# A two-block float32 transformer on one core: rounded products of four stages walk their 272 columns in pieces instead of in order

## The chip, the cores and the metric

The kernel runs on one core of a Trainium2 chip. The metric is the time of one execution on the device in microseconds (us). Before the change the median of two runs is 1358.34 us (1358.07 to 1358.61).

## The reference, cut to what matters

Two transformer blocks of two layers each run over the same 272 tokens (16 meta tokens and 256 of the input), with 1024 features. All operands are float32.

```python
h = concatenate([meta, x])                       # 272 x 1024
for i in range(2):                               # first block
    h = h + (gla_mixer, dsa_mixer)[i](rmsnorm(h, norm_mix[i]), ...)
    h = h + swiglu(rmsnorm(h, norm_ffn[i]), ffn_w_in[i], ffn_w_out[i])
x = rmsnorm(h, norm_final)[:, 16:]
h = concatenate([meta_2, x])                     # second block, again 272 tokens
h = h + retention_mixer(rmsnorm_2(h, g), ret_w_in, ...)
h = h + swiglu_2(rmsnorm_2(h, g), w1, w3, w2)
h = h + mla_mixer(rmsnorm_2(h, g), ..., k_shared, v_shared)
h = h + swiglu_2(rmsnorm_2(h, g), w1, w3, w2)
out = rmsnorm_2(h, final_g)[:, 16:]
```

Nearly all the arithmetic is in projections `hn @ w`, where `hn` is a normed 272 x 1024 matrix, and in the products of the feed-forward layers (hidden size 2816).

## The kernel before

**Layout.** Activations are kept with features on the 128 partitions and tokens along the columns: `xx` holds a normed input as eight tiles (`k` = 0 to 7) of 128 features by 272 tokens, and `aa` holds second operands (the input of an output projection, the hidden state of a feed-forward layer) in the same way. A tile's row is 320 elements long, of which 272 are used.

**Split products.** Every float32 factor `v` is split into a rounded part `hi` (type fp32r) and a rest `lo = v - hi`, also rounded. `Split` names the two halves of such a pair. A product is then three matmuls for each `k` that add into the same PSUM bank: `hi` weights by `hi` columns (line 589), `hi` weights by `lo` columns (line 590), `lo` weights by `hi` columns (line 591). In each the 128x128 weights are the stationary operand (tiles `uh` and `ul`) and the 272 tokens are the moving one. This is `product`. A *unit* is eight such weight tiles, 128 output features in all; one call of `product` takes one unit, so it issues 24 matmuls of 272 columns. A product with only `hi` weights (unit 0, lines 568 and 570) is a special case. In two feed-forward layers (`PAIRED`, f = 1 and 3) lines 584 and 586 take `hi` and `lo` columns in one matmul of 512: line 586 reads two runs of 256 columns that lie far apart, line 584 reads 512 columns that lie next to each other.

**Stages.** `norm_x(i)` is the `Split` of the i-th normed input. In order of time:

- i = 0: the projections of gated linear attention (GLA), `chunk` over gate, keys, queries, values and r;
- i = 1: `ffn(0, ...)`, 22 columns of units for the gate and 22 for the up projection;
- i = 2 and 3: sparse attention (DSA) and its feed-forward layer, with 256 columns in most products;
- i = 4: the projections of retention: 16 for queries and keys, 16 for values, 16 for the gate;
- i = 5: `ffn(2, ...)`, 44 units;
- i = 6 and 7: latent attention (MLA) and the last feed-forward layer, with 256 columns.

Of these, i = 0, 1, 4 and 5 take all 272 columns. The second product of each feed-forward layer reads `aa` through `ffn_y(f)`.

**Order and queues.** Each engine's program is written out by hand, in one block per engine. Weights come from HBM on SyncE's queue into three `raw` buffers; ScalarE rounds them into `uh` (line 1188), VectorE subtracts into `ul` (line 1785). Four PSUM banks (`lin`) take the products in turn, four more (`aux`) the small ones. VectorE or ScalarE empties a bank (line 1797, for instance) once the last matmul of its product has raised the semaphore `s_mm`, and `take` makes TensorE wait for that before the bank is used again. No semaphore is raised within a product, so nothing reads a bank between its 24 matmuls.

**What the change touches.** The class `Split`, the function `norm_x`, and in `product` the three matmuls of lines 589 to 591:

```python
e.matmul(ps[:, 0:n1 - n0], hi[:, k, :], x.hi[:, k0 + j, n0:n1], start=first and j == 0, stop=False)
e.matmul(ps[:, 0:n1 - n0], hi[:, k, :], x.lo[:, k0 + j, n0:n1], start=False, stop=False)
i = e.matmul(ps[:, 0:n1 - n0], lo[:, k, :], jh[k0 + j] if x.joined else x.hi[:, k0 + j, n0:n1], ...)
```

Small products that the rows below speak of: line 917 is the attention output of one head (plain float32; three products, the last of which writes two runs of 64 PSUM columns that lie 128 apart), line 992 is a score product of retention (plain float32).

Of the kernel before, what the change touches and what calls it, by code (L numbers as in the profile page):

```python
# [56 lines left out]
class Seen:  # L57


    def __init__(self, e):  # L60
        self.e, self.top = e, {}
# [46 lines left out]
class Split:  # L108


    def __init__(self, pair, s_hi, s_lo, base=0, joined=False):
        self.joined = joined
        self.pair, self.hi, self.lo = pair, pair[:, 0], pair[:, 1]
        self.s_hi, self.s_lo, self.base = s_hi, s_lo, base


def build(nc, A, out):
    ctx = ExitStack()
    with ctx:
# [3 lines left out]
        def sem(name):  # L123
            return ctx.enter_context(nc.semaphore(name))
# [10 lines left out]
        _, xx, xx_flat = parts_of("xx", KC)  # L135
# [4 lines left out]
        joined = [xx_flat[:, 2 * ROW * k + GAP_X:2 * ROW * k + GAP_X + 2 * TQ] for k in range(KC)]  # L140
        jh, jl = [j[:, 0:TQ] for j in joined], [j[:, TQ:2 * TQ] for j in joined]
# [29 lines left out]
        class Arena:  # L171
            def __init__(self):
                self.at = 0
# [319 lines left out]
        s_hi, s_lo, s_pad = sem("s_hi"), sem("s_lo"), sem("s_pad")  # L493
# [8 lines left out]
        s_xh, s_xl, s_sq, s_ssq = ([sem(f"{n}{i}") for i in range(8)] for n in ("s_xh", "s_xl", "s_sq", "s_ssq"))  # L502
# [28 lines left out]
                             "s_res1", "s_out", "s_qs"))  # L531

        def norm_x(i):
            return Split(xx, s_xh[i], s_xl[i], 0, i == 7)

        def ffn_y(i):
            return Split(aa, s_fh, s_fl, FC * i)
# [14 lines left out]
        def _(e):  # L552
            w = Seen(e)
            n_mm = n_ax = 0

            def product(ps, x, n0, n1, k0=0, first=True, last=True, part=None, pair=False, ahead=0):

                nonlocal n_mm  # L560
                u = len(unit_end) + ahead
                hi, lo = unit_hi(u), unit_lo(u)
                ks = range(unit_n(u)) if part is None else part
                if u in PACKED:
                    w.wait_ge(s_lo, u + 1)
                    for k in ks:
                        w.wait_ge(x.s_hi, x.base + k + 1)
                        e.matmul(ps[:, 0:n1 - n0], hi[:, k, :], x.hi[:, k, n0:n1], start=k == 0, stop=False)
                        w.wait_ge(x.s_lo, x.base + k + 1)
                        i = e.matmul(ps[:, 0:n1 - n0], hi[:, k, :], x.lo[:, k, n0:n1], start=False, stop=k == KC - 1)  # L570
                    i.then_inc(s_mm, 1)
                    n_mm += 1
                    unit_end.append(n_mm)
                    return
                if u != HALVED:
                    w.wait_ge(s_hi, u + 1)
                    w.wait_ge(s_lo, u + 1)
                for j, k in enumerate(ks):
                    if u == HALVED:
                        w.wait_ge(*((s_lo, u + 1) if k >= 4 else (s_lo_half, 1)))  # L580
                    w.wait_ge(x.s_hi, x.base + k0 + j + 1)
                    w.wait_ge(x.s_lo, x.base + k0 + j + 1)
                    if pair and x.joined:
                        e.matmul(ps[:, :], hi[:, k, :], joined[k0 + j], start=first and j == 0, stop=False)  # L584
                    elif pair:
                        e.matmul(ps.rearrange("p (a n) -> p a n", a=2), hi[:, k, :], x.pair[:, :, k0 + j, n0:n1],  # L586
                                 start=first and j == 0, stop=False)
                    else:
                        e.matmul(ps[:, 0:n1 - n0], hi[:, k, :], x.hi[:, k0 + j, n0:n1], start=first and j == 0, stop=False)  # L589
                        e.matmul(ps[:, 0:n1 - n0], hi[:, k, :], x.lo[:, k0 + j, n0:n1], start=False, stop=False)  # L590
                    i = e.matmul(ps[:, 0:n1 - n0], lo[:, k, :], jh[k0 + j] if x.joined else x.hi[:, k0 + j, n0:n1],  # L591
                                 start=False, stop=last and j == len(ks) - 1)
                i.then_inc(s_mm, 1)
                n_mm += 1
                if part is None or ks[-1] == unit_n(u) - 1:
                    unit_end.append(n_mm)
# [62 lines left out]
            def small(key, by, steps=1):  # L659
                return aux.take(w, key, by, steps)  # L660
# [60 lines left out]
            ps = small("gain0", "D")  # L721
# [13 lines left out]
            for k in range(KC):  # L735
# [3 lines left out]
                ps = (lin if k < 4 else aux).bank(key)  # L739
                w.wait_ge(s_x[k // 4], 32)  # L740
                for n in (1, 2):
                    i = turned(ps, k, n)
# [8 lines left out]
            x = norm_x(0)  # L751
# [48 lines left out]
            ps = small(("n", 0), "D")  # L800
# [4 lines left out]
            ps = small("gain1", "D")  # L805
# [11 lines left out]
            for s in range(16):  # L817
                if s == 10:

                    ps = lin.take(w, ("gr", 2), "D")  # L820
# [31 lines left out]
            x = norm_x(2)  # L852
# [70 lines left out]
            for c in range(4):  # L923
                chunk(("di", c), "D", x, NM, T)
                if c == 0:
                    ps = small("dw8", "D")
                    w.wait_ge(s_dki, 1)
                    for b in range(2):
                        i = e.transpose(ps[:, b * P:(b + 1) * P], d_wT[:, b * P:(b + 1) * P], ident)
# [41 lines left out]
            x = norm_x(4)  # L971
# [93 lines left out]
            x = norm_x(6)  # L1065
# [55 lines left out]
            x = norm_x(7)  # L1121
            together([(3, "g", 0), (3, "g", 1)], x, NM, T, None, True)
            total(("n", 7), "A", s_ssq[7], KC - 1, ssq[0], TQ)
            ps = small("tokens", "A")
            for b in range(2):
                i = e.matmul(ps[:, b:b + 1], ssq[0][:, b * P:(b + 1) * P], ones[:, 0:1], start=True, stop=True)
# [1760 lines left out]
```

## Time and profile before

| | |
|---|---|
| median of two runs | 1358.34 us (1358.07 to 1358.61) |
| span of the profiled execution, first to last instruction | 1356.6 us |
| TensorE matmul busy | 1350.0 us, 100% |
| TensorE weight load busy | 1289.1 us, 95% |
| VectorE, ScalarE, GpSimd busy | 1010.7, 709.1, 295.4 us |
| granted TensorE clock, mean | 0.999 of full speed |
| read from HBM | 226.80 MB, 168 GB/s over the span |

The profiled execution has its span and no separate time; the runs lie 1.5 to 2.0 us above that span, and their median 1.74 us.

The profile's rows name the engine (PE is a TensorE matmul, PEld its weight load, DVE is VectorE, ACT ScalarE, POOL GpSimd), the line of the kernel, the operation, output and input tiles, shapes, and count. Busy time counts each instruction from start to end. Matmuls overlap in the pipeline, so that a row's duration (0.29 us) is much longer than the time from one start to the next (0.12 us); it is the starts that tell the rate.

### The profile page before, as it was taken

What the parts mean: (1) busy time and instruction counts of PE and PEld (TensorE: products, weight loads), DVE (VectorE), ACT (ScalarE), POOL (GpSimd) and SP (SyncE); (2) the same over time, 40 slices, a digit from 0 to 9 for tenths busy, and PEclk for the clock granted to TensorE, in tenths of its full rate; (3) what the DMA queues carried; (4) which work ended last, traced back from release to release, by engine and by line L of the source; (5) the groups of instructions that cost most, each with busy time, mean ns of one, the idle gap of its engine ahead of it and who ended that gap; (6) DMA issues with size and microseconds to landing.
All of it is one profiled execution on the core that took longest, in us unless ns stands there. A gap on an engine that the chain in (4) does not pass through costs nothing.

```text
span 1356.6 us, 24729 instructions
## 1 busy us (share of the span) xinstructions
PE 1350.0 (100%) x9873; PEld 1289.1 (95%) x9873; DVE 1010.7 (75%) x1613; ACT 709.1 (52%) x1167; POOL 295.4 (22%) x313
## 2 busy tenths in 40 slices
PE   9999999999999999999999999999999999999998
PEld 9999999999999888899999999999999999988886
DVE  6788766656987988778877876766557885898843
ACT  7565544434756555544444664544435565655543
POOL 1136000023152000132355744000023533120000
PEclk9999999999999999999999999999999999999999
DMA  8334665665443655565543455555554553566552
GB/s 279 125 125 158 191 192 185 190 186 162 136 157 126 214 190 194 170 197 181 163 134 125 155 186 158 185 174 171 170 172 150 183 161 121 172 199 189 189 184 77
DMA packets 220457, 229.72 MB, mean 169 GB/s; under 512 B 13664, under 2 KB 207704, under 8 KB 220344
## 3 DMA queue, kind: packets, MB, share of 16 engines
q1 hardware_dynamic: 219232, 226.24, 52.1%
q10 hardware_dynamic: 1112, 1.90, 0.6%
q8 instruction: 80, 1.31, 0.4%
q14 instruction: 33, 0.27, 0.1%
HBM read 226.80 MB, written 1.33 MB: 168 GB/s over the span
## 4 chain that ended last, share of the span: by engine, by line
PE 99%; DMA 0%; issue 0%; DVE 0%; ACT 0%; ACTq 0%; DVEq 0%
PE ps L591 28%; PE ps L589 21%; PE ps L590 20%; PE ps L586 8%; PE ps L584 6%; PE ps L1148 2%; PE ps L1147 2%; PE ps L1146 1%; PE ps L650 1%; PE ps L649 1%; PE ps L651 1%; PE ps L917 1%; PE ps L787 1%; PE ps L992 1%; PE ps L775 0%; PE ps L1080 0%
## 5 line engine op out<-in xcount | busy, mean ns | idle before, releaser
L1188 ACT ACTIVATE uh<-raw 128x1024 fp32r<-128x1024 f32 (+4 forms) x452 | 446.8, 999 | 441.4 <-PE ps L591 380.5
L1785 DVE TENSOR_TENSOR ul<-raw,uh 128x1024 fp32r<-128x1024 f32 (+3 forms) x448 | 529.8, 1190 | 132.7 <-PE ps L591 84.6
L591 PE MATMUL ps<-xx,ul 128*128 128x272 f32 (+1 forms) x2136 | 609.3, 285 | 0.0
L589 PE MATMUL ps<-xx,uh 128*128 128x272 f32 (+1 forms) x1448 | 422.8, 292 | 0.0
L590 PE MATMUL ps<-xx,uh 128*128 128x272 f32 (+1 forms) x1448 | 413.8, 286 | 0.0
L591 PEld LDWEIGHTS ps<-xx,ul 128*128 128x128 f32 x2136 | 401.3, 188 | 0.0
L589 PEld LDWEIGHTS ps<-xx,uh 128*128 128x128 f32 x1448 | 272.3, 188 | 3.0 <-issue 1.7
L590 PEld LDWEIGHTS ps<-xx,uh 128*128 128x128 f32 x1448 | 272.6, 188 | 0.8
L591 PE MATMUL ps<-aa,ul 128*128 128x272 f32 (+1 forms) x920 | 260.6, 283 | 0.0
L589 PE MATMUL ps<-aa,uh 128*128 128x272 f32 (+1 forms) x788 | 228.6, 290 | 0.0
L590 PE MATMUL ps<-aa,uh 128*128 128x272 f32 (+1 forms) x788 | 226.7, 288 | 0.0
L591 PEld LDWEIGHTS ps<-aa,ul 128*128 128x128 f32 x920 | 173.6, 189 | 0.0
L589 PEld LDWEIGHTS ps<-aa,uh 128*128 128x128 f32 x788 | 148.0, 188 | 1.0 <-issue 0.7
L590 PEld LDWEIGHTS ps<-aa,uh 128*128 128x128 f32 x788 | 148.0, 188 | 0.2
L584 PE MATMUL ps<-xx,uh 128*128 128x512 f32 x352 | 123.7, 394 | 0.0
L586 PE MATMUL ps<-xx,uh 128*128 128x512 f32 x352 | 122.8, 394 | 0.0
L1797 DVE TENSOR_TENSOR tmp<-ps,rbc 128x272 f32<-128x272 f32 x112 | 49.0, 439 | 81.0 <-PE ps L591 80.5
L2590 POOL TENSOR_TENSOR ssq<-h 128x272 f32<-128x272 f32 (+1 forms) x5 | 7.5, 1496 | 428.0 <-DVE h L1826 294.9
L586 PEld LDWEIGHTS ps<-xx,uh 128*128 128x128 f32 x352 | 66.1, 188 | 15.5
L584 PEld LDWEIGHTS ps<-xx,uh 128*128 128x128 f32 x352 | 66.1, 188 | 15.2
L1876 DVE TENSOR_REDUCE tmp<-ps 128x256 f32<-128x512 f32 x88 | 60.6, 689 | 20.8 <-PE ps L591 19.1
L2590 POOL TENSOR_TENSOR sqt<-h 128x272 f32<-128x272 f32 (+1 forms) x25 | 39.3, 1572 | 84.4 <-DVE h L1826 61.5
(345 smaller groups left out, 1706.5 us busy)
## 6 DMA issues: line engine op xcount, KB each, us to landing
raw<-in_ffn_w SPq DMA_DIRECT2D x62, 1024.0 KB, 5.3
raw<-in_ffn_w_in SPq DMA_DIRECT2D x44, 1024.0 KB, 5.2
raw<-in_ret_w_in SPq DMA_DIRECT2D x24, 1024.0 KB, 5.1
raw<-in_ffn_w_out SPq DMA_DIRECT2D x16, 1024.0 KB, 5.6
raw<-in_gla_w_in SPq DMA_DIRECT2D x11, 1024.0 KB, 5.1
raw<-in_ret_w_o SPq DMA_DIRECT2D x8, 1024.0 KB, 5.2
raw<-in_dsa_w_in SPq DMA_DIRECT2D x7, 1024.0 KB, 5.6
raw<-in_ffn_w_out SPq DMA_DIRECT2D x8, 768.0 KB, 4.9
```

The source lines that it names most:

```text
L584: e.matmul(ps[:, :], hi[:, k, :], joined[k0 + j], start=first and j == 0, stop=False)
L586: e.matmul(ps.rearrange("p (a n) -> p a n", a=2), hi[:, k, :], x.pair[:, :, k0 + j, n0:n1], start=first and j == 0, stop=False)
L589: e.matmul(ps[:, 0:n1 - n0], hi[:, k, :], x.hi[:, k0 + j, n0:n1], start=first and j == 0, stop=False)
L590: e.matmul(ps[:, 0:n1 - n0], hi[:, k, :], x.lo[:, k0 + j, n0:n1], start=False, stop=False)
L591: i = e.matmul(ps[:, 0:n1 - n0], lo[:, k, :], jh[k0 + j] if x.joined else x.hi[:, k0 + j, n0:n1], start=False, stop=last and j == len(ks) - 1)
L1147: e.matmul(ps[:, :], y.hi[:, k, tokens], lo[:, j, :], start=False, stop=False)
L1148: m = e.matmul(ps[:, :], y.lo[:, k, tokens], hi[:, j, :], start=False, stop=k == FC - 1)
L1188: i = e.activation(unit_hi(u)[:, :, cols], a, ACT.Copy)
L1785: i = e.tensor_tensor(unit_lo(u)[:, :, cols], a, unit_hi(u)[:, :, cols].bitcast(F32), ALU.subtract)
L1797: e.tensor_tensor(dst, lin.bank(key)[:, 0:T - n0], rbc[:, n0:T], ALU.mult).then_inc(lin.empties(key, "D"), 1)
L1876: e.tensor_reduce(t, lin.bank(key).rearrange("p (a n) -> p n a", a=2), AX, ALU.add).then_inc(lin.empties(key, "D"), 1)
L2590: e.tensor_tensor(sq if k else total, src, src, ALU.mult).then_inc(s_ssq[i], 1)
```

## The change

`Split` gets a field `walk`, which `norm_x` sets for i = 0, 1, 4 and 5. A new function `walked` views the 272 columns as pieces in another order. Both the moving operand and the PSUM output of lines 589 to 591 are viewed so; each column therefore still lands in its own place in PSUM, and only the order in which the columns are visited within one matmul is new.

- i = 0, `("halves", 8)`: pieces of 8 columns, alternately from the first 136 columns and from the last 136, 34 pieces;
- i = 1, `("turns", 4)`: pieces of 4; first the even ones, then the odd ones, 68 pieces;
- i = 4, `("back", 16)`: 17 pieces of 16, the last piece first, each read forwards;
- i = 5, `("turns", 34)`: 8 pieces of 34, the even ones first.

Unit 0, the paired products, the products of 256 columns and all that read `aa` stay in order (their `walk` is `None`).

```diff
-    def __init__(self, pair, s_hi, s_lo, base=0, joined=False):
-        self.joined = joined
+    def __init__(self, pair, s_hi, s_lo, base=0, joined=False, walk=None):
+        self.joined, self.walk = joined, walk
...
         def norm_x(i):
-            return Split(xx, s_xh[i], s_xl[i], 0, i == 7)
+            return Split(xx, s_xh[i], s_xl[i], 0, i == 7, {0: ("halves", 8), 1: ("turns", 4), 4: ("back", 16), 5: ("turns", 34)}.get(i))
...
+            def walked(v, walk):
+
+                if walk is None:
+                    return v
+                kind, q = walk
+                if kind == "turns":
+                    return v.rearrange("p (n c q) -> p c n q", c=2, q=q)
+                if kind == "halves":
+                    return v.rearrange("p (c n q) -> p n c q", c=2, q=q)
+                return v.rearrange("p (n q) -> p n q", q=q)[:, ::-1, :]
...
                     else:
-                        e.matmul(ps[:, 0:n1 - n0], hi[:, k, :], x.hi[:, k0 + j, n0:n1], start=first and j == 0, stop=False)
-                        e.matmul(ps[:, 0:n1 - n0], hi[:, k, :], x.lo[:, k0 + j, n0:n1], start=False, stop=False)
-                    i = e.matmul(ps[:, 0:n1 - n0], lo[:, k, :], jh[k0 + j] if x.joined else x.hi[:, k0 + j, n0:n1],
+                        to = walked(ps[:, 0:n1 - n0], x.walk)
+                        e.matmul(to, hi[:, k, :], walked(x.hi[:, k0 + j, n0:n1], x.walk), start=first and j == 0,
+                                 stop=False)
+                        e.matmul(to, hi[:, k, :], walked(x.lo[:, k0 + j, n0:n1], x.walk), start=False, stop=False)
+                    i = e.matmul(walked(ps[:, 0:n1 - n0], x.walk), lo[:, k, :],
+                                 jh[k0 + j] if x.joined else walked(x.hi[:, k0 + j, n0:n1], x.walk),
                                  start=False, stop=last and j == len(ks) - 1)
```

TensorE's queue has the same instructions in the same order; only their shapes differ. In `ffn(0, ...)`, where the total of the squares (line 673) stands between two products of the first gate units, TensorE's rows before are:

```order
L589 MATMUL ps<-xx,uh 128x272
L590 MATMUL ps<-xx,uh 128x272
L591 MATMUL ps<-xx,ul 128x272
L673 MATMUL ps<-ssq,ones 128x272
L589 MATMUL ps<-xx,uh 128x272
L590 MATMUL ps<-xx,uh 128x272
```

and with the change (line numbers grow by 12 to 14) they are:

```order
L601 MATMUL ps<-xx,uh 128x2x34x4
L603 MATMUL ps<-xx,uh 128x2x34x4
L604 MATMUL ps<-xx,ul 128x2x34x4
L687 MATMUL ps<-ssq,ones 128x272
L601 MATMUL ps<-xx,uh 128x2x34x4
L603 MATMUL ps<-xx,uh 128x2x34x4
```

Nothing moved: 2x34x4 are two turns of 34 pieces of 4 columns, and the sum of squares keeps its 272 columns in order. Where the products of `ffn(1, ...)` end (they read `aa`) and the first product of retention begins (it reads `xx`), TensorE had before:

```order
L589 MATMUL ps<-aa,uh 128x256
L590 MATMUL ps<-aa,uh 128x256
L591 MATMUL ps<-aa,ul 128x256
L589 MATMUL ps<-xx,uh 128x272
L590 MATMUL ps<-xx,uh 128x272
L591 MATMUL ps<-xx,ul 128x272
```

and has now:

```order
L601 MATMUL ps<-aa,uh 128x256
L603 MATMUL ps<-aa,uh 128x256
L604 MATMUL ps<-aa,ul 128x256
L601 MATMUL ps<-xx,uh 128x17x16
L603 MATMUL ps<-xx,uh 128x17x16
L604 MATMUL ps<-xx,ul 128x17x16
```

Again only the shape is new, 17 pieces of 16 columns, and the products that read `aa` are as they were.

## Rows read from the trace of the kernel before

**Rows 1.** The page: busy time by engine; the chain that ended last.

```profile
PE 1350.0 (100%) x9873; PEld 1289.1 (95%) x9873; DVE 1010.7 (75%) x1613; ACT 709.1 (52%) x1167; POOL 295.4 (22%) x313
...
PE 99%; DMA 0%; issue 0%; DVE 0%; ACT 0%; ACTq 0%; DVEq 0%
PE ps L591 28%; PE ps L589 21%; PE ps L590 20%; PE ps L586 8%; PE ps L584 6%; PE ps L1148 2%; PE ps L1147 2%; PE ps L1146 1%; PE ps L650 1%; PE ps L649 1%; PE ps L651 1%; PE ps L917 1%; PE ps L787 1%; PE ps L992 1%; PE ps L775 0%; PE ps L1080 0%
```

**Rows 2.** Waits of TensorE, whole span: us in total, times, longest us.

```profile
PE ps L717 <- DVE small L1925: 1.0, 1, 1.0
PE ps L1006 <- issue: 0.2, 1, 0.2
```

**Rows 3.** Stages i = 0, 1, 4, 5 by windows: length; busy time (count) by engine.

```profile
core 0: us, PE busy (x) PEld busy (x) DVE busy (x) ACT busy (x) POOL busy (x), PEclk, DMA share, GB/s
11.90:106.10 94.20, 94.20 (x746) 91.35 (x745) 77.00 (x125) 61.70 (x102) 17.96 (x23) 1.00 0.50 164
130.10:263.10 133.00, 133.00 (x1064) 132.03 (x1063) 89.97 (x135) 64.47 (x94) 3.74 (x9) 1.00 0.60 189
615.90:789.90 174.00, 173.84 (x1385) 172.61 (x1384) 143.60 (x229) 84.22 (x142) 86.01 (x83) 1.00 0.45 147
837.80:969.70 131.90, 131.90 (x1061) 131.77 (x1060) 89.62 (x134) 63.56 (x91) 5.15 (x11) 1.00 0.55 174
```

**Rows 4.** Groups by shape: the rounded matmuls of 272 columns on `xx`.

```profile
L589 PE MATMUL ps<-xx,uh 128*128 128x272 f32 x1304 | 380.0, 291 | 0.0
L591 PE MATMUL ps<-xx,ul 128*128 128x272 f32 x1304 | 375.5, 288 | 0.0
L590 PE MATMUL ps<-xx,uh 128*128 128x272 f32 x1304 | 373.4, 286 | 0.0
```

**Rows 5.** TensorE's timeline in stage i = 5: start us, length us, instruction.

```profile
899.62 0.29 PE L590 MATMUL ps<-xx,uh 128*128 128x272 f32 x1
899.75 0.29 PE L591 MATMUL ps<-xx,ul 128*128 128x272 f32 x1
...
902.99 0.29 PE L590 MATMUL ps<-xx,uh 128*128 128x272 f32 x1
```

**Rows 6.** Timeline of the paired products: line 586 twice (f = 1), line 584 (f = 3).

```profile
439.65 0.40 PE L586 MATMUL ps<-xx,uh 128*128 128x512 f32 x1
...
441.42 0.40 PE L586 MATMUL ps<-xx,uh 128*128 128x512 f32 x1
...
479.94 0.39 PE L586 MATMUL ps<-xx,uh 128*128 128x512 f32 x1
...
481.33 0.39 PE L586 MATMUL ps<-xx,uh 128*128 128x512 f32 x1
...
1199.62 0.40 PE L584 MATMUL ps<-xx,uh 128*128 128x512 f32 x1
...
1201.73 0.40 PE L584 MATMUL ps<-xx,uh 128*128 128x512 f32 x1
```

**Rows 7.** Line 917, all records: duration min/median/max, first and last start.

```profile
L917 PE MATMUL ps<-arena x96: 272/275/379, 388.6 to 1152.6; 128*128 128x128 f32 x64, 128*128 128x256 f32 x32
```

**Rows 8.** Timeline around plain float32 matmuls of 272 columns (line 992).

```profile
644.81 1.08 PE L992 MATMUL ps<-arena 128*128 128x272 f32 x4
645.53 0.49 PE L589 MATMUL ps<-xx,uh 128*128 128x272 f32 x1
645.86 0.29 PE L590 MATMUL ps<-xx,uh 128*128 128x272 f32 x1
```

## The prediction, made before the changed kernel had run

> **What bounds the kernel now.** I read the page's busy times and chain first. TensorE's matmuls cover 1350.0 of 1356.6 us and the chain that ended last is TensorE for 99% of its length [rows 1]. The list of waits then says that TensorE waits 1.2 us in all, at the very start and once in retention [rows 2]. So no transfer, no rounding on ScalarE, no subtraction on VectorE and no emptying of a bank is late anywhere: the time is the number of matmuls times the distance from one start to the next. The reader should not take "busy 100%" as "at its peak", though. Busy time counts a record of 0.29 us whole, while the next one starts 0.12 us later.
>
> The third view, the windows by stage, gives the share of the change: the four stages that it touches last 94.2, 133.0, 174.0 and 131.9 us, together 533.1 us or 39% of the span, all at the full granted clock (1.00, the level of 2.4 GHz) [rows 3]. The fourth, the timeline, gives the distance. From 899.62 to 902.99 us lie 27 matmuls, 3.37 us / 27 = 124.8 ns each [rows 5]; the whole stage says the same, 131.9 us for 1056 such matmuls and a few others, under 125 ns each [rows 3]. I take 125 ns. At one column per cycle of 2.4 GHz the 272 columns would stream in 113.3 ns, so 11.7 ns of each distance are something else, and the trace doesn't say what.
>
> **The change, part by part.** Nothing is added, removed or moved in any queue. What is new is the order of columns within a matmul, for `norm_x` of 0, 1, 4 and 5.
>
> *Count.* A unit is 8 `k` by 3 lines, 24 matmuls. Stage 0 has 4 units of keys, 4 of queries, 8 of values and 8 of r: 24 x 24 = 576. Stage 1 has 44 units, 1056; stage 4 has 16 + 16 + 16 = 48, 1152; stage 5 has 44, 1056. Together 3840. The groups by shape confirm it: 1304 on each of the three lines [rows 4], less 24 each of the three DSA units with 272 columns, is 1280, and 3 x 1280 = 3840. The pieces are 576 x 34 = 19,584 in stage 0, 1056 x 68 = 71,808 in stage 1, 1152 x 17 = 19,584 in stage 4 and 1056 x 8 = 8,448 in stage 5, 119,424 in all. More than half are in stage 1.
>
> *Around the matmul.* All 24 matmuls of a product visit the columns in the same order, so the distance in time between two additions to one PSUM column stays a whole matmul, 125 ns. Readers wait for the last matmul of the product, which needs all columns whatever their order, so nothing that VectorE or ScalarE does comes earlier or later. Should TensorE be quicker, VectorE has room: in its fullest stage of the four it is busy 143.6 of 174.0 us [rows 3]. These parts cost nothing because nothing in them changes, not because something hides them. TensorE has no cover at all: one nanosecond more on each of the 3840 matmuls is 3.84 us on the end.
>
> *Price of a jump.* No rounded matmul of the trace has short pieces, so I bound the price.
> - Two runs against one: line 586 reads 256 columns and then 256 far away; line 584 reads 512 in a row. A pair of that matmul and the 256-column one of line 591 takes (441.42 - 439.65) / 5 = 354 ns in one place of line 586 and (481.33 - 479.94) / 4 = 347.5 ns in another, and (1201.73 - 1199.62) / 6 = 351.7 ns on line 584 [rows 6]. The two places with a jump lie on either side of the one without: a single jump of the moving operand costs nothing that can be told from the level on which a stretch happens to run. These two levels, 6.5 ns apart with equal shapes, are my measure of what an order of accesses can do by itself.
> - Split output: line 917 writes 256 columns, 128 in a row, and then 128 as two runs of 64. Its 64 records of 128 columns, half of them split, have 272 ns at least and 275 ns in the middle [rows 7]. One jump in PSUM costs at most 3 ns. These are plain float32 matmuls, which take two records and so leave memory more time per column, so this is the weaker witness.
> - Below nothing: at most the 11.7 ns that aren't streaming could go, 3840 x 11.7 = 45 us. That would be the end of the scale on the fast side, 1313 us.
> - Above: the slowest use of 272 columns in the trace is half rate. The plain float32 matmuls of line 992 together with one rounded one take 645.86 - 644.81 = 1.05 us, so (1.05 - 0.125) / 4 = 231 ns each [rows 8], 106 ns more than 125. On all 3840 that is 407 us. It is the far end, and I see no reason why pieces of 16 or 34 columns should run like that.
>
> I take the nearest rows, which are those with jumps in rounded matmuls [rows 6]: no price per jump, a level more or less by chance. One level of 6.5 ns per group of three matmuls (1280 groups) is 8.3 us; two levels either way, 17 us, are the forecast's own range, about 1341 to 1375 us.
>
> *A rule that speaks against it.* By row, the split output of line 917 is not slower than its contiguous neighbour by more than 3 ns [rows 7]. The Trainium skill, page Advanced Engine Details and Errata, section PSUM Cachelines, says otherwise in its first line: "Any non-contiguous AP significantly slows down matmuls". Its next line, and the section on SBUF cachelines, are milder: PSUM lines hold two float32 values and want pairs of neighbours, SBUF lines are 16 bytes and want two hits each. By the milder lines every piece here is harmless, since all lengths and starts are even; they are also the only ones that the trace agrees with. By the first line the four stages would be slower by an amount that the page doesn't give; what such a slowdown would be here is the third rival, priced from rows.
>
> *Sum.* 1356.6 us of the profiled span + 0 = 1356.6 us, and 1.74 us from the span to the median of the runs, 1358.3 us.
>
> **Rivals.**
> - *Jumps cost a cycle.* TensorE's address generator, or the memory behind it, loses one column slot of 2.4 GHz (0.417 ns) at every piece. Place: all four stages, in proportion to pieces. Price: 119,424 x 0.417 ns = 50 us, 30 of it in stage 1, giving 1408 us. For it: 11.7 ns per matmul are already lost to something. Against: one jump in line 586 doesn't show, though 0.4 ns could hide in the levels of 6.5 ns. It decides (over 2%, 27 us) from 0.23 ns a piece. With a slot at 1.2 GHz instead it would be 100 us, 1458 us.
> - *Short pieces halve the rate.* Memory serves neighbours in larger units, or in alternating banks; "even ones first" with pieces of 4 then uses half of each unit or always the same bank, and stage 1 runs as line 992 does: 1056 x 106 ns = 112 us, 1470 us. If stage 0 with its pieces of 8 joins, 61 us more, 1531 us. For it: the order looks like the worst one for such a memory. Against: no row shows it, and pieces of 4 still bring four neighbours at a time.
> - *A better order.* The 11.7 ns come from collisions of the column stream with the weight loads or with the writes of VectorE, which a new order avoids. The two levels in rows 6 say that such things exist. For over 2% each of the 3840 matmuls would have to win 7.1 of the 11.7 ns under all four walks; 1330 us would be typical. The levels are worth 6.5 ns per three matmuls or per pair, so I doubt it.
> - *The walks don't reach the chip.* If the build put the pieces in order again, nothing would change; the shapes that I see (2x34x4) speak against it, and the time would be the forecast's.
>
> **How the numbers follow.** The forecast (no price, with the levels) gets 0.68; it holds the case of walks that do nothing. A cycle per jump gets 0.12 (1408 us, or more for a slower slot), halved rate 0.15 (1470 us and up), a better order 0.05 (1330 us). A measurement of this kernel can tell about 2%, 27 us, from no change. So faster by over 2% is 0.05, slower 0.27, between them 0.68. The range begins at 1335 us, a level below the forecast's own, and ends at 1410 us, where it takes in the cheap jump at 1408. That leaves out the halved rate, 0.15, and the larger part of the better order, below 0.2 together. The forecast's own range stays 1341 to 1375 us.
>
> **What would show it.** In the timeline of stage 5, 27 matmuls in 3.37 us as before, and the same in stage 1, where the difference should be largest; the windows of the four stages should last 94, 133, 174 and 132 us. A cycle per jump would show as 125 + 68 x 0.417 = 153 ns between starts in stage 1, 139 in stage 0, 132 in stage 4 and 128 in stage 5, in proportion to pieces. A halved rate would show as 231 ns in stage 1 and little in stages 4 and 5. If instead one stage alone is longer and its pieces aren't the shortest, what matters is alignment or direction, and my reasoning by pieces is wrong. If TensorE shows new waits, the idea that nothing else is touched is wrong.

## The result, and the profile after the change

The changed kernel takes 1373.64 us (median of two runs, 1373.52 to 1373.76) against 1358.34 us: ratio 1.0113, 95% interval 1.0096 to 1.0129. That is 15.3 us more. The forecast was no change, 1358.3 us; the time lies within its range of 1335 to 1410 us, even within the forecast's own 1341 to 1375, but the kernel did become slower, clear of noise, and the forecast had named no cause for that. The range was drawn for chance levels and for a price per jump, neither of which is what came, so that the time fell inside it is luck.

The profiled execution's span is 1371.7 us. The same four stages in windows, from the first to the last matmul that the change touches (length; busy time and count of PE, PEld, DVE, ACT, POOL; clock; DMA share; GB/s), the kernel before first:

```profile
core 0: us, PE busy (x) PEld busy (x) DVE busy (x) ACT busy (x) POOL busy (x), PEclk, DMA share, GB/s
11.93:106.09 94.16, 94.16 (x745) 91.31 (x744) 76.96 (x125) 61.66 (x102) 17.95 (x23) 1.00 0.50 164
130.12:263.09 132.97, 132.97 (x1063) 132.00 (x1062) 89.95 (x135) 64.45 (x94) 3.72 (x9) 1.00 0.60 189
615.88:789.92 174.04, 173.88 (x1386) 172.65 (x1385) 143.64 (x229) 84.26 (x142) 86.05 (x83) 1.00 0.45 147
837.84:969.56 131.72, 131.72 (x1059) 131.59 (x1058) 89.62 (x134) 63.56 (x91) 5.15 (x11) 1.00 0.55 174
```

and the changed kernel:

```profile
11.78:109.61 97.83, 97.83 (x745) 94.94 (x744) 77.87 (x125) 62.61 (x103) 17.54 (x23) 1.00 0.48 158
133.64:266.68 133.04, 133.04 (x1064) 132.06 (x1062) 90.02 (x135) 64.46 (x94) 3.71 (x9) 1.00 0.61 188
619.47:795.92 176.45, 176.35 (x1386) 175.19 (x1384) 144.22 (x230) 85.10 (x143) 86.88 (x83) 1.00 0.44 145
843.84:984.74 140.90, 140.90 (x1059) 140.90 (x1058) 89.82 (x134) 63.58 (x91) 5.14 (x11) 1.00 0.52 163
```

This view settles where the time went. Stage 0 is longer by 3.67 us, stage 1 by 0.07, stage 4 by 2.41 and stage 5 by 9.18, 15.3 us in all, and the rest of the span moved by no more than 0.2 us. The stage with by far the most and shortest pieces (stage 1, 68 pieces of 4) pays nothing; the one with the fewest and longest (stage 5, 8 pieces of 34) pays most.

The rows that answer to [rows 4] and [rows 5] are these groups and this piece of TensorE's timeline in stage 5:

```profile
L601 PE MATMUL ps<-xx,uh 128*128 128x272 f32 x1304 | 384.7, 295 | 0.0
L604 PE MATMUL ps<-xx,ul 128*128 128x272 f32 x1304 | 380.7, 292 | 0.0
L603 PE MATMUL ps<-xx,uh 128*128 128x272 f32 x1304 | 379.9, 291 | 0.0
```

```profile
899.41 0.29 PE L603 MATMUL ps<-xx,uh 128*128 128x272 f32 x1
...
903.01 0.29 PE L603 MATMUL ps<-xx,uh 128*128 128x272 f32 x1
...
903.41 0.29 PE L603 MATMUL ps<-xx,uh 128*128 128x272 f32 x1
```

There are 27 matmuls from 899.41 to 903.01, 133.3 ns each, where there were 124.8. The groups show the same counts, the same shape (it prints 128x272 for any order of columns) and records that are 4 to 5 ns longer, which is the mean over all stages (15.3 us / 3840 is 4.0 ns). A learner who looks at the groups alone can't see that one stage pays nothing and another 9 ns. From here on "the distance" is the time from one start to the next, a third of the time over three matmuls in a row, as a mean over all such groups of a stage or part that no other instruction interrupts. The kernel before has 124.45 ns in stages 1 and 5 (124.6 and 124.8 in stages 0 and 4), and the changed one about 131 in stage 0, 124.5 in stage 1, 127.2 in stage 4 and 133.3 in stage 5.

### The profile page after: what moved, and what is told of

It is laid out like the page before. It is cut to its first block, busy times and chain, and to the rows that moved or that the text cites. A ratio compares the mean times of both kernels' runs of the same rounds, so it can differ in the third digit from the quotient of the medians.

```text
span 1371.7 us, 24729 instructions
## 1 busy us (share of the span) xinstructions
PE 1363.5 (99%) x9873; PEld 1303.0 (95%) x9873; DVE 1011.3 (74%) x1613; ACT 709.2 (52%) x1167; POOL 293.4 (21%) x313
## 4 chain that ended last, share of the span: by engine, by line
PE 99%; DMA 0%; SPq 0%; issue 0%; DVE 0%; ACT 0%; DVEq 0%
PE ps L604 28%; PE ps L601 21%; PE ps L603 21%; PE ps L597 8%; PE ps L595 6%; PE ps L1162 1%; PE ps L1161 1%; PE ps L1160 1%; PE ps L664 1%; PE ps L663 1%; PE ps L665 1%; PE ps L931 1%; PE ps L801 1%; PE ps L1006 1%; PE ps L789 0%; PE ps L1094 0%
## 5 line engine op out<-in xcount | busy, mean ns | idle before, releaser
L601 PE MATMUL ps<-xx,uh 128*128 128x272 f32 (+1 forms) x1448 | 427.4, 295 | 0.0
L603 PE MATMUL ps<-xx,uh 128*128 128x272 f32 (+1 forms) x1448 | 420.3, 290 | 0.0
L604 PE MATMUL ps<-aa,ul 128*128 128x272 f32 (+1 forms) x920 | 263.5, 286 | 0.0
```

The costliest lines, as they stand in the source:

```text
L601: e.matmul(to, hi[:, k, :], walked(x.hi[:, k0 + j, n0:n1], x.walk), start=first and j == 0, stop=False)
L603: e.matmul(to, hi[:, k, :], walked(x.lo[:, k0 + j, n0:n1], x.walk), start=False, stop=False)
L604: i = e.matmul(walked(ps[:, 0:n1 - n0], x.walk), lo[:, k, :], jh[k0 + j] if x.joined else walked(x.hi[:, k0 + j, n0:n1], x.walk), start=Fa ...
```

## The experiments

In all of them the walk is a table by stage, a stage can be split into equal parts by unit (so one kernel holds up to 14 walks), and a walk can be applied to the moving operand or to PSUM alone:

```diff
-                    i = e.matmul(walked(ps[:, 0:n1 - n0], x.walk), lo[:, k, :],
+                    i = e.matmul(walked(ps[:, 0:n1 - n0], walk, "write"), lo[:, k, :],
...
+                if walk is None or walk[2] not in ("both", side):
+                    return v
```

Where a part is a quarter of stage 1 or 5 (264 matmuls), its window, from first to last start, holds 263 distances, so length / 263 is the distance. The first quarter of each stage and all parts of stages 0 and 4 also hold other instructions; for those the starts are read.

### Reading or writing?

```diff
-WALKS = {0: [("halves", 8, "both")], 1: [("turns", 4, "both")], 4: [("back", 16, "both")], 5: [("turns", 34, "both")]}
+WALKS = {0: [("halves", 8, "read")], 1: [("turns", 4, "read")], 4: [("back", 16, "read")], 5: [("turns", 34, "read")]}
```

> Only the moving operand is read in the four walks; PSUM is written in order (so each product lands in other columns than the reference's). In the changed kernel the mean distance between starts was 131.0 ns in stage 0 (pieces of 8 from two halves), 124.5 in stage 1 (pieces of 4 in two turns), 127.1 in stage 4 (16 backwards) and 133.3 in stage 5 (34 in two turns), against 124.4 before. Theory R (the cost lies in reading the moving operand): the same four numbers, 1373 us. Theory W (it lies on the PSUM side): 124.4 in all four stages, 1358 us. If both sides have to jump together (theory J), less than the sum in both this run and the next.

and the same with "write":

> Only PSUM is written in the four walks; the moving operand is read in order (columns land in other places than the reference's). Theory R: 124.4 ns in all four stages, 1358 us. Theory W: 131.0, 124.5, 127.1 and 133.3 ns, 1373 us. Theory J: less than that.

Reading alone took 1373.93 us, writing alone 1358.31 us, beside 1358.36 us of the kernel before on that chip. The windows, reading first:

```profile
12.20:110.04 97.84, 97.84 (x745) 94.96 (x744) 77.58 (x125) 62.02 (x102) 17.55 (x23) 1.00 0.48 155
134.07:267.11 133.04, 133.04 (x1064) 132.07 (x1062) 90.02 (x135) 64.44 (x94) 3.71 (x9) 1.00 0.61 189
619.90:796.36 176.46, 176.36 (x1386) 175.20 (x1385) 144.23 (x230) 85.13 (x143) 86.88 (x83) 1.00 0.45 145
844.28:985.18 140.90, 140.90 (x1059) 140.90 (x1058) 89.75 (x134) 63.54 (x91) 5.14 (x11) 1.00 0.52 163
```

```profile
11.89:106.04 94.15, 94.15 (x745) 91.29 (x744) 76.99 (x125) 62.09 (x103) 17.92 (x23) 1.00 0.51 163
130.07:263.04 132.97, 132.97 (x1063) 132.00 (x1062) 89.99 (x135) 64.44 (x94) 3.73 (x9) 1.00 0.61 189
615.83:789.88 174.05, 173.89 (x1386) 172.66 (x1385) 143.65 (x229) 84.28 (x142) 86.02 (x83) 1.00 0.45 147
837.80:969.52 131.72, 131.72 (x1059) 131.59 (x1058) 89.62 (x134) 63.56 (x91) 5.15 (x11) 1.00 0.56 174
```

The four stages have the lengths of the changed kernel in the one and of the kernel before in the other, to 0.01 us. The whole price is in reading the moving operand from SBUF. (Each side jumped alone here, so products land in other columns than they should; the arithmetic per matmul is the same.) PSUM takes pieces of 4, 8, 16 and 34 columns in these orders for nothing.

### The walk or the stage?

The walks change places (stage 0 gets pieces of 4, stage 1 of 34, stage 4 of 8 from two halves, stage 5 16 backwards).

> The same four walks in other stages, both sides: stage 0 pieces of 4 in turns, stage 1 pieces of 34 in turns, stage 4 pieces of 8 from two halves, stage 5 pieces of 16 backwards. If the walk sets the price: 124.5, 133.3, 131.0 and 127.1 ns; against before 0 + 1056 x 8.9 + 1152 x 6.6 + 1056 x 2.7 ns = 20 us, 1378 us. If the stage sets it (its neighbours on other engines): 131, 124.5, 127 and 133 ns as in the changed kernel, 1373 us.

It took 1377.59 us, where the first theory said 1378. Stages 1 and 5 of this run:

```profile
130.52:272.84 142.32, 142.32 (x1064) 141.33 (x1062) 90.12 (x135) 64.39 (x94) 3.72 (x9) 1.00 0.57 178
854.27:988.82 134.55, 134.55 (x1060) 134.52 (x1059) 89.66 (x134) 63.55 (x91) 5.14 (x11) 1.00 0.55 171
```

Stage 1 with pieces of 34 is 9.35 us longer than before and stage 5 with 16 backwards 2.83 us; stage 4 with the two halves is 6.67 us longer (131.0 ns). The price goes with the walk, not with what the other engines do in the stage, to within about 1 ns: stage 0 with pieces of 4, for which nothing was expected, is 0.49 us longer (125.5 against 124.6 ns), and 16 backwards adds 2.8 ns in stage 5 where it added 2.4 in stage 4.

### Other sizes

(`"both"` is left out here.)

```diff
+WALKS = {0: [("halves", 4), ("halves", 34)], 1: [("turns", 2), ("turns", 8)],
+         4: [("back", 4), ("back", 8), ("back", 34), ("back", 68)], 5: [("turns", 68), ("back", 136)]}
```

> Other sizes, both sides. Stage 0: halves 4, then halves 34; stage 1: turns 2, then turns 8; stage 4: backwards 4, 8, 34, 68; stage 5: turns 68, then backwards 136. Theory C (a price for pieces whose ends cut a group of four neighbouring columns): halves 34 and backwards 34 cost like turns 34 (some 9 ns), turns 2 costs most (every group of four is cut), 4, 8, 68 and 136 cost nothing. Theory D (a price for far jumps, whatever the ends): halves 4 costs twice halves 8 (some 13 ns), backwards 4 costs more than backwards 16, turns 2 and turns 8 nothing, as turns 4.

It took 1429.40 us. The two halves of stage 1 (turns 2, turns 8), and a stretch of TensorE's timeline with 34 backwards:

```profile
133.48:263.39 129.91, 129.91 (x535) 110.09 (x534) 46.90 (x69) 33.66 (x50) 3.72 (x9) 1.00 0.32 99
263.63:328.91 65.28, 65.28 (x529) 65.27 (x528) 43.39 (x66) 30.91 (x44) 0.00 (x0) 1.00 0.60 188
```

```profile
812.56 0.30 PE L620 MATMUL ps<-xx,uh 128*128 128x272 f32 x1
...
814.22 0.30 PE L620 MATMUL ps<-xx,uh 128*128 128x272 f32 x1
```

Pieces of 2 take some 244 ns, twice the time in order; pieces of 8 in two turns take 65.28 us / 527 = 123.9 ns, a little less than in order. Backwards, 34 has 12 matmuls in 1.66 us, 138 ns. The other distances: halves 4 and halves 34 130.4 and 130.3, backwards 4 124.6, backwards 8 127, backwards 68 126, backwards 136 126.7, turns 68 124.6. So theory C is right that a cut group of four costs, though not with one price (it said some 9 ns for every walk with pieces of 34; they add 6, 9 and 13), and theory D fails in its main claim (halves 4, with twice the jumps of halves 8, costs the same). But halves 4 and most backward walks cost something without any cut, so C isn't all.

### Where a piece starts

The same walks, but started at column 0, 2, 1 or 4, reading only. Each is an access pattern of its own:

```diff
+                if kind == "ap":
+                    return bass.AP(v.tensor, v.offset + q[0], [v.ap[0]] + [list(d) for d in q[1]])
...
+5: [four(0), four(2), four(1), four(4)]     # four(o) = ("ap", (o, ((0, 2), (8, 34), (1, 4))), "read")
```

> Read side only; parts of the columns are read twice and others left out, so that the same walk can start at column 0, 2, 1 or 4; PSUM in order. Theory C (the moving operand is read in groups of four neighbouring columns that start at multiples of 4, and each visit of a group takes 4 column times whatever part of it is used): the distance follows the visits of groups per matmul, as turns 2 (136 visits, 244 ns) and in order (68 visits, 124.4 ns) say, 1.76 ns a visit. Stage 5: pieces of 4 at every eighth column, twice: from column 0, 124 ns; from 2, 244; from 1, 244; from 4, 124. Stage 4: pieces of 8 at every sixteenth column, twice: from 0, 124; from 2 (102 visits), 184; from 4, 124; from 1, 184. Stage 1: two runs of 136: from 0, 124; from 2 (70 visits), 128; two different runs from 0, 124; from 1, 128. Theory S (two columns of a group are enough for full speed, what costs is very short pieces): stages 4 and 1 stay at 124 throughout, and stage 5 too apart from starts 1 and 2.

Stage 5, its quarters from columns 0, 2, 1 and 4:

```profile
873.37:906.54 33.17, 33.17 (x267) 33.06 (x266) 24.16 (x34) 17.22 (x25) 5.15 (x11) 1.00 0.53 161
906.67:972.09 65.42, 65.42 (x265) 54.77 (x264) 22.10 (x34) 15.45 (x22) 0.00 (x0) 1.00 0.31 97
972.35:1036.32 63.97, 63.97 (x264) 54.75 (x263) 22.10 (x34) 15.44 (x22) 0.00 (x0) 1.00 0.30 91
1036.56:1069.34 32.78, 32.78 (x265) 32.75 (x263) 21.29 (x32) 15.44 (x22) 0.00 (x0) 1.00 0.51 164
```

One walk, one length of pieces, one number of jumps: 65.42 / 263 = 248.7 ns when each piece takes two columns from each of two groups of four, 243.2 when it starts at 1 (three columns and one), and 124.6 when it starts at a multiple of 4. In stage 4 pieces of 8 have 176 ns from column 2 and 173 from 1 (expected 184) and about 125 from 0 and 4. In stage 1 two runs of 136 have 130.3 ns from 2, 128.9 from 1 and 124.5 from 0. Stage 0 holds the walk that is nearest to the changed kernel's stage 5, four runs of 68: from column 0 it has 126.6 ns, from column 2, with the same jumps and 72 visits, 133.5. In this stretch, from column 2, 18 distances take 2.41 us:

```profile
60.50 0.30 PE L630 MATMUL ps<-xx,uh 128*128 128x272 f32 x1
...
62.91 0.30 PE L630 MATMUL ps<-xx,uh 128*128 128x272 f32 x1
```

The time rises with the visits to groups of four, but not with one price: 2 more visits add 4.3 to 5.7 ns, 4 more 6.9, 34 more 48 to 51 (1.5 ns each, where theory C's own price of 1.76 ns had led to 184 ns), 68 more 119 to 124 (1.8 ns each). Theory S, by which two columns of a group are enough, is out by stages 4 and 1.

### Two places at once, and one place for ever

```diff
+D = lambda d: ("ap", (0, ((4, 34), (d, 2), (1, 4))), "read")     # pieces of 4, alternately from two streams d columns apart
+1: [D(8), D(16), D(32), D(64)], 5: [D(96), D(128), D(132), D(136)], 0: [("ap", (0, ((0, 68), (1, 4))), "read"), ...]
```

> Read side only, pieces of 4 that all begin at multiples of 4 (68 visits), alternately from two streams D columns apart; stage 1: D = 8, 16, 32, 64; stage 5: D = 96, 128, 132, 136. Theory B (two places far apart collide in memory by their distance): single values of D stand out, 131 ns at D = 136 as halves 4 had, 124 at others. Theory F (any alternation between two places costs, by leaving the order): 131 ns for all D from 16 up. Stage 4: backwards 16 and backwards 4 by another way (expected 127 and 126 ns as before), then in order by the same kind of view (124.4), then the first 16 columns 17 times; stage 0: one group of four 68 times, then each group twice. If the 11 ns beyond 113.3 come from a collision within the column stream, the repeats fall to about 116 ns; if from something outside the stream, they stay at 124.

The quarters with D = 16, 32 and 64 (stage 1), 128, 132 and 136 (stage 5):

```profile
163.23:197.13 33.90, 33.90 (x265) 33.90 (x264) 22.09 (x34) 15.48 (x22) 0.00 (x0) 1.00 0.60 177
197.26:231.45 34.19, 34.19 (x266) 34.19 (x264) 22.09 (x34) 15.46 (x22) 0.00 (x0) 1.00 0.58 179
231.58:267.51 35.93, 35.93 (x266) 35.93 (x264) 21.30 (x32) 15.54 (x22) 0.00 (x0) 1.00 0.60 185
...
878.41:914.34 35.93, 35.93 (x265) 35.93 (x264) 22.10 (x34) 15.59 (x22) 0.00 (x0) 1.00 0.54 170
914.48:950.30 35.82, 35.82 (x265) 35.82 (x264) 22.09 (x34) 15.60 (x22) 0.00 (x0) 1.00 0.49 151
950.45:984.74 34.29, 34.29 (x265) 34.29 (x264) 21.30 (x32) 15.47 (x22) 0.00 (x0) 1.00 0.55 176
```

These are 128.9, 130.0, 136.6, 136.6, 136.2 and 130.4 ns, all with whole groups and 68 visits. Every alternation costs some 5 ns (theory F), and some distances 12 (theory B); each theory was half right. In stage 4, 16 backwards, 4 backwards and in order, written as access patterns, came out at 127.1, 125.2 and 125.0 ns, so the way a walk is written isn't what costs. In stage 0 one group of four was read 68 times by each matmul:

```profile
39.83 0.28 PE L630 MATMUL ps<-xx,uh 128*128 128x272 f32 x1
...
41.80 0.28 PE L633 MATMUL ps<-xx,ul 128*128 128x272 f32 x1
43.69 0.41 PE L734 MATMUL ps<-cst,tmp 128*128 128x128 f32 x2 [1.61 <-DVE tmp L1847]
```

That is 17 distances in 1.97 us, 115.9 ns, 2.6 above the 113.3 of one column per cycle. The second half of stage 0 was meant to read each group twice in a row, but its pattern, `(0, 34), (4, 2), (1, 4)`, reads the first 8 columns 34 times: groups 0, 1, 0, 1 and so on, another group at every visit. It has the same distance, 12 in 1.39 us, 115.8 ns:

```profile
58.41 0.28 PE L630 MATMUL ps<-xx,uh 128*128 128x272 f32 x1
...
59.80 0.28 PE L630 MATMUL ps<-xx,uh 128*128 128x272 f32 x1
```

The first 16 columns 17 times gave 128.0. So the 11 ns that the prediction left unexplained depend on the stretch of columns that the stream reads: they nearly vanish for a stream that stays within 4 or 8 columns. It isn't the change of group by itself that takes them, and what does stays open. The row of L734 is a lesson by the way: at this speed TensorE runs out of work once and waits 1.61 us for VectorE.

### Do the weight loads take part?

```diff
+                def W(a, k):
+                    if walk is None or len(walk) < 4:
+                        return a[:, k, :]
+                    return ones_r[:, :] if walk[3] == "ones" else a[:, 0, :]
```

> The weights of some products are read from one fixed tile (ones_r, all ones) or from the first of the unit's eight, so those products are not the reference's. Theory L (the column stream collides with the loads of the next weights, and the walk only changes where): with a fixed tile in order falls from 124.4 towards 116 ns, and halves 8 and backwards 16 lose the 6.6 and 2.7 ns that they add. Theory N (weights have no part): in order 124.4, halves 8 131, turns 34 133.3, backwards 16 127 ns with either tile. Turns 2 stays at 244 ns under both. Stage 0: turns 8 (123.9 ns before) and halves 68 (a far jump at every 68 columns, no cut: 124 to 125 ns).

Stage 1: the weights from the first of eight tiles in order (second quarter), then halves 8 with the fixed tile and with the first of eight:

```profile
164.27:197.00 32.73, 32.73 (x265) 32.73 (x264) 22.09 (x34) 15.46 (x22) 0.00 (x0) 1.00 0.62 182
197.13:231.60 34.47, 34.47 (x265) 34.47 (x264) 22.10 (x34) 15.46 (x22) 0.00 (x0) 1.00 0.58 180
231.74:266.22 34.48, 34.48 (x266) 34.48 (x264) 21.30 (x32) 15.45 (x22) 0.00 (x0) 1.00 0.62 190
```

124.4, 131.1 and 131.1 ns; turns 34 had 132.2 and 133.3, backwards 16 126.7 and 127.2, turns 2 again some 244. For these walks the tile from which the weights come matters by 1.1 ns at most. It is not so for turns 8: in stage 4, with the fixed tile, it has 126.3 ns on average, where every other run has 123.8 to 123.9, and for most of that quarter 126.6 (18 distances in 2.28 us here):

```profile
821.34 0.30 PE L630 MATMUL ps<-xx,ones_r 128*128 128x272 f32 x1
...
823.62 0.30 PE L630 MATMUL ps<-xx,ones_r 128*128 128x272 f32 x1
```

So theory L fails in what it forecast, a fall towards 116 ns in order and walks that lose their price. That the loads play a part isn't excluded: they were aimed elsewhere, never taken away. That the loads alone don't set the 124.4 ns is shown by e6, where the same loads stand before matmuls of 115.9 ns. Halves 68 came out at 125.7 in stage 0 and turns 8 at 123.9.

### Is there a better order?

Here "(c, q)" means c turns of pieces of q: the first turn takes the pieces 0, c, 2c and so on, the next begins at piece 1.

> Both sides, orders that cut no group of four, all of 68 visits: in c turns of pieces of q. Stage 1: (4 turns, pieces of 4), (17, 4), (34, 4), (2, 8); stage 5: (17, 8), (2, 68), halves 68, backwards 8; stage 4: (2, 8), (4, 4), (17, 4), in order; stage 0: (2, 8), (4, 4). Theory of this point (one price per visit of a group, plus a price for orders that alternate between two places): all but the last two of stage 5 at 124 to 125 ns, since each goes forward in equal steps; halves 68 and backwards 8 at 126 to 127. Rival (memory has some 16 parts that take turns by address; an order that comes back to one part soon collides): steps of 4 groups (4 turns of 4) 128 ns, 17 groups (17 turns of 4) about as in order, 34 groups (34 turns of 4: two visits a turn) 130 ns.

It took 1360.99 us. The quarters of stage 1 (4, 17 and 34 turns of pieces of 4, 2 turns of 8) and the first of stage 5 (17 turns of 8, 268 records with some others):

```profile
129.54:163.52 33.98, 33.98 (x271) 33.01 (x270) 24.50 (x35) 18.01 (x28) 3.72 (x9) 1.00 0.58 186
163.65:196.52 32.87, 32.87 (x266) 32.87 (x264) 22.10 (x34) 15.46 (x22) 0.00 (x0) 1.00 0.61 182
196.64:230.93 34.29, 34.29 (x266) 34.29 (x264) 22.09 (x34) 15.47 (x22) 0.00 (x0) 1.00 0.58 181
231.06:263.63 32.57, 32.57 (x266) 32.57 (x264) 21.30 (x32) 15.44 (x22) 0.00 (x0) 1.00 0.65 198
...
837.45:872.17 34.72, 34.72 (x268) 34.72 (x267) 24.25 (x34) 17.26 (x25) 5.15 (x11) 1.00 0.50 154
```

By groups of three they are 122.9, 125.0, 130.4, 123.8 and 131.1 ns. The orders with 34 and (pieces of 8) 17 turns come back to a place 136 columns away every second piece: written out, they are the walks halves 4 and halves 8 of before, and cost the same 130.4 and 131.1. The other orders of stage 1, which go forward in equal steps, cost 0.5 ns or gain a little. My point theory said 124 to 125 for all of them and fails for these two, as e4 and the changed kernel had already shown. In the rest of stage 5, (2, 68) and halves 68, again one walk under two names, have 125.6 both, and backwards 8 127.8. In e4 that same walk of pieces of 68 had 124.6, with three matmuls at a steady 373 ns for most of its half, where e8 has 373 to 380 in a repeating series. One walk can thus run on two levels 1 ns apart, which is as much as the smallest differences read here. The rival fails as well: it said 128 for 4 turns of 4, the best of all.

> Only stage 5 keeps its walk (pieces of 34), the other three are back in order. If the stages add up without touching each other: 1056 x (133.3 - 124.45) = 9.3 us above the kernel before, 1367.7 us, and 6.0 us below the changed kernel. If the stages influence each other (what a stage starts on decides its level): off that by more than 1 us.

1367.47 us, ratio 1.0070 (1.0056 to 1.0083). Stage 5 is as long as in the changed kernel and the other three are as before, so the stages add up:

```profile
839.23:980.14 140.91, 140.91 (x1059) 140.91 (x1058) 89.78 (x134) 63.57 (x91) 5.14 (x11) 1.00 0.52 163
```

Then three versions that keep every result in its place and were meant to beat both kernels:

> All four stages visit pieces of 8 columns, even ones first. Run e4 had 123.85 ns for it in half of stage 1 against 124.45 in order. If that holds everywhere: 3840 x 0.6 ns = 2.3 us below the kernel before, 1356.0 us. If stages differ (stage 0 had 124.5 with it in e7, in its first half): between 1356 and 1359 us.

1356.11 us, ratio 0.9982 (0.9973 to 0.9991); 1356.0 was expected, and the distance is 123.8 to 123.9 ns in all four stages.

> Two turns of pieces of 8 in all unpaired rounded products, those on aa and those of 256 columns too (2016 more matmuls of 272 columns on aa, some 400 of 256, and the third matmul of the pairs of f = 1). If the 0.6 ns of a matmul hold for them: another 1.2 us below e9, 1354.9 us. If the gain depends on where a tile lies in memory (aa lies elsewhere than xx): between 1353 and 1358 us.

1354.99 us, ratio 0.9974 (0.9965 to 0.9984). The 1354.9 us expected came out by luck: the gain was put on the products of 272 columns on `aa`, and they gained nothing (124.5 ns in e9, 124.6 here). What got shorter are products of 256 columns, on `xx` from 119.2 to 117.1 ns and on `aa` from 117.8 to 117.5; the pairs that line 586 begins went from 347.7 to 350.0 ns on `xx` and from 350.0 to 346.7 on `aa`.

> All four stages in four turns of 17 pieces of 4 columns. Run e8 had 123.3 ns for it in a quarter of stage 1, against 123.8 for two turns of pieces of 8 and 124.45 in order. If that holds everywhere: 3840 x 1.1 ns = 4.2 us below the kernel before, 1354.2 us. If the price depends on the level on which a stretch runs (the sums for three matmuls lay between 361 and 373 ns there): up to 4 ns a matmul below, 1350 us, or nothing.

```diff
+                if kind == "grid":
+                    return v.rearrange("p (n c q) -> p c n q", c=q[0], q=q[1])     # (4, 4) in stages 0, 1, 4 and 5
```

1352.37 us, ratio 0.9955 (0.9942 to 0.9969), 6.2 us under the 1358.55 us of the kernel before on that chip and 21 us under the changed kernel. Expected were 4.2 us, from 123.3 ns; the distance is 122.9 to 123.0 ns in all four stages, 1.5 to 1.9 less than in order. Stages 1 and 5:

```profile
129.25:260.63 131.38, 131.38 (x1064) 130.41 (x1062) 90.02 (x135) 64.37 (x94) 3.73 (x9) 1.00 0.62 191
833.29:963.49 130.20, 130.20 (x1059) 130.04 (x1058) 89.66 (x134) 63.50 (x91) 5.15 (x11) 1.00 0.56 176
```

A table of numbers in an access pattern, with no instruction more or fewer and every result in its place, thus moves this kernel between 1352 us and 1429 us (e11 and e4).

## Why the prediction was wrong, point by point

- **What bounds the kernel**: right. TensorE alone, with no cover: a longer distance between starts went to the end in full, and TensorE's list of waits names none within the four stages.
- **Count**: right, and the runs confirm it by their sums (e10: 1056 x 8.85 ns = 9.3 us expected, 9.2 us in the window and 8.9 us in the medians).
- **Around the matmul**: right. No reader was affected, and writing in the new order cost nothing (e2).
- **Price of a jump**: this is the step that failed. I took "no price per jump" from line 586, whose one jump per matmul lies between whole groups of four, and carried it to all pieces by their count. Count of jumps is the wrong unit. What is paid for first is a visit to a group of four columns: 68 visits take 124.4 ns, 136 take 243 to 249. In order or in turns of 4 there are 68. A piece of 34 begins or ends in the middle of a group and touches 9, so stage 5 has 8 x 9 = 72. The nearest control, runs of 68 with and without cut groups, puts 6.9 ns on 4 more visits (e5); by it some 7.3 of stage 5's 9.2 us are an estimate for cut groups. It is no more than that, since halves 34, turns 34 and backwards 34 have 72 visits each and stand some 5, 8 to 9 and 12 ns above the same walks with pieces of 68. The rest of stage 5, some 2 ns, and all of stages 0 and 4 is a second price, for the order of the visits: 6.4 ns for going to and fro between the halves, 2.4 for 16 backwards. The forecast had 0 for both terms; 15.3 us were measured for the two together, of which some 7.3 us by this estimate for cut groups and 8.0 us for order. The first is explained, the second only located: it arises where the moving operand is read (e1, e2).
- **The levels**: they misled. I saw 347.5 and 354 ns with equal shapes, called it chance, and allowed two levels either way. They are no chance: a stage's length repeats from run to run to 0.01 us, and in both kernels the pairs of line 586 begin at 346 ns, go to 354 after one long pair (541 ns) and back to 347 after another (456 ns). Nor are they a measure of what an order does, since there the level changes with the order unchanged.
- **The rule of the Trainium skill**: the sentence of the Trainium skill, page Advanced Engine Details and Errata, section PSUM Cachelines ("Any non-contiguous AP significantly slows down matmuls"), is contradicted here, by less than 0.1 us for four walks on the PSUM side (e2). The pairs that its next line wants were always whole, so that one was not tested. The section SBUF Cachelines of that page of the Trainium skill was nearer to the point than I allowed: its lines of 16 bytes are as long as the groups of four float32 columns. But two hits on a line, which it says are needed, are not enough here: with two of four columns used per visit the matmul takes twice as long (pieces of 2: 244 ns). Because of it I wrote that every piece is harmless "since all lengths and starts are even". To cut no group they would have to be multiples of 4, and even then the order can cost.
- **Rivals**: a cycle per jump is refuted by stage 1, 124.5 ns where it said 153. "Short pieces halve the rate" had the right mechanism, memory that serves neighbours in larger units, and the wrong unit: with 4 columns instead of 8 or more it reaches pieces of 2 and 34, not those of 4. I had 0.15 on it and 1470 us. Its price, the 231 ns of line 992, wasn't the far end either: pieces of 2 take 244 ns and pieces of 4 from column 2 249. "A better order" came true in its effect (e11), for other orders than these; that it avoids collisions with weight loads or writes is not shown.
- **What would show it**: the sentence that a longer stage without the shortest pieces would mean alignment or direction described what came. I should have made a rival of it: with four columns as the unit and 8 x 9 visits at 124.4 / 68 = 1.83 ns, the estimate for stage 5 would have been 7.3 ns per matmul, 7.7 us, before the run.

**Still open.** What makes one order of whole groups dearer than another was mapped but not explained: to and fro costs 5 ns at most distances and 12 at 64, 128 and 132 columns; four turns of 4 gain 1.5; 34 backwards (138 ns) costs more than 34 in turns (133.3) or from two halves (130.3) with 72 visits each; `aa` gains nothing from an order that helps `xx`; turns 8 loses its gain with weights from the fixed tile. Nor is it known why 4 or 8 columns again and again take 115.9 ns and 16 take 128. A model with some 16 parts of memory failed on its first test (e8). Where the columns lie in SBUF, and products without weight loads between them, were not varied; both may enter here.

## What to carry to other kernels

When TensorE is the only bound, count for each matmul how many aligned groups of four float32 columns its moving operand touches, not how many pieces it has: cut groups are paid for every time. Jumps between whole groups can be free (68 pieces of 4 in two turns), but not in every order: to and fro between two places cost 5 to 12 ns per matmul. The PSUM side took these orders free. Read the distance between starts by stage: a group's mean, 4 ns up here, hid a stage with nothing and one with 9 ns. And a row with one jump per instruction is a witness for that jump only; look where it begins and ends before carrying it over.

## What the runs showed of the hardware that I had not expected

- The rounded product reads 272 columns in 124.4 ns, and the same matmul that stays within the first 4 or 8 columns takes 115.9 ns, within the first 16 128.0 (e6). Most of what separates this kernel's matmuls from one column per cycle of 2.4 GHz thus depends on the stretch of columns that is read.
- Half of each group used means about half the speed: 244 ns for pieces of 2.
- Two streams 64 or 128 columns apart cost 136.6 ns, 32 or 136 apart 130.
- Four turns of pieces of 4 are quicker than reading in order, 123.0 against 124.45 ns, and brought 0.45% of the whole kernel.
